# Moving the sums of an FFN's down weight blocks from one engine's queue to another's

## The reference, cut to what matters

```
def conv_ffn(x, norm_g, w_up, conv_w, conv_b, w_down):
    u = rmsnorm(x, norm_g) @ w_up                  # 256 x 5632
    ... # causal convolution of width 3 over positions
    val, gate = jnp.split(c, 2, axis=-1)
    return (jax.nn.silu(gate) * val) @ w_down      # (256 x 2816) @ (2816 x 1024)
```

## Time and profile before

| | us |
|---|---|
| median of 3 runs | 949.56 (948.84 to 949.63) |
| the profiled execution, its own time | 948.84 |
| its span, first to last instruction | 947.0 |
| PE busy | 936.0 (99%) |
| DVE busy | 799.8 (84%) |
| ACT busy | 278.2 (29%) |
| POOL busy | 0.7 (0%) |

### The profile page before, as it was taken

One profiled execution on the slowest core, in us unless ns is written; L12 is line 12 of the kernel. 1 busy time (PEld: TensorE's weight loads), 2 busy tenths in 40 slices (PEclk: granted clock), 3 DMA queues, 4 the chain that ended last, 5 costly groups with the idle time before them and its releaser, 6 DMA issues.

```text
span 947.0 us, 16131 instructions
## 1 busy us (share of the span) xinstructions
PE 936.0 (99%) x6456; PEld 865.2 (91%) x6456; DVE 799.8 (84%) x1822; ACT 278.2 (29%) x622; POOL 0.7 (0%) x7
## 2 busy tenths in 40 slices
PE   9999999999999999999999999999999999999997
PEld 7888999999999998889999999999888878888876
DVE  4778879999998878777699999988799985899953
ACT  1033122221212111263122221220424563624561
POOL 0000000000000000000000000000000000000000
PEclk9999999999999999999999999999999999999999
DMA  8942455363634650757254545446933428443101
GB/s 312 411 184 105 178 187 218 153 254 147 264 140 160 231 209 3 282 195 305 94 224 171 230 180 221 181 161 241 341 133 98 159 94 297 156 149 110 32 1 45
DMA packets 36859, 171.80 MB, mean 181 GB/s; under 512 B 5032, under 2 KB 8880, under 8 KB 23344
## 3 DMA queue, kind: packets, MB, share of 16 engines
q1 hardware_dynamic: 35120, 167.72, 47.7%
q10 hardware_dynamic: 1664, 3.04, 0.9%
HBM read 169.69 MB, written 2.64 MB: 182 GB/s over the span
## 4 chain that ended last, share of the span: by engine, by line
PE 92%; DVE 3%; DMA 2%; ACT 1%; issue 0%; ACTq 0%; SPq 0%; DVEq 0%
PE bank L1355 26%; PE bank L1375 15%; PE bank L1039 9%; PE bank L1458 5%; PE bank L1692 4%; PE bank L1108 3%; PE bank L1331 3%; PE bank L1301 3%; PE bank L1115 3%; PE bank L1678 3%; PE bank L1554 2%; PE bank L1573 2%; PE bank L1051 1%; PE bank L1498 1%; PE bank L1624 1%; DMA ring<-in_ring 1%
## 5 line engine op out<-in xcount | busy, mean ns | idle before, releaser
L1375 PE MATMUL bank<-work,fring 128*128 128x128 f32 x1008 | 115.5, 275 | 0.0
L1375 PEld LDWEIGHTS bank<-work,fring 128*128 128x128 f32 x1008 | 114.0, 192 | 0.0
L2514 DVE SCALAR_TENSOR_TENSOR work<-work,cols 128x256 f32<-128x256 f32 x240 | 98.8, 477 | 1.0 <-ACT work L893 0.5
L1355 PE MATMUL bank<-sq,fring 128*128 128x128 f32 x640 | 84.5, 275 | 0.0
L724 ACT ACTIVATE work<-work,cols 128x256 f32<-128x256 f32 x88 | 47.8, 593 | 111.0 <-DVE work L2237 96.2
L1355 PE MATMUL bank<-ring,fring 128*128 128x128 f32 x640 | 78.1, 275 | 0.0
L1355 PE MATMUL bank<-sq,ring 128*128 128x128 f32 x640 | 78.0, 275 | 0.0
L1355 PEld LDWEIGHTS bank<-sq,fring 128*128 128x128 f32 x640 | 77.9, 192 | 0.0
L1355 PEld LDWEIGHTS bank<-ring,fring 128*128 128x128 f32 x640 | 74.8, 192 | 0.2
L1355 PEld LDWEIGHTS bank<-sq,ring 128*128 128x128 f32 x640 | 74.7, 192 | 0.0
L2256 DVE SCALAR_TENSOR_TENSOR work<-work,cols 128x256 f32<-128x256 f32 x176 | 71.5, 477 | 0.0
(11 more groups left out here) (420 smaller groups left out, 1724.7 us busy)
## 6 DMA issues: line engine op xcount, KB each, us to landing
ring<-in_ring SPq DMA_DIRECT2D x60, 1024.0 KB, 6.9
fring<-in_up SPq DMA_DIRECT2D x44, 1024.0 KB, 6.8
ada_w<-in_ada SPq DMA_DIRECT2D x48, 512.0 KB, 6.3
fring<-in_down SPq DMA_DIRECT2D x44, 512.0 KB, 4.5
ring<-in_ring SPq DMA_DIRECT2D x2, 800.0 KB, 6.5
bias_skewed<-bias_rows SPq DMA_DIRECT2D x1, 1536.0 KB, 13.1
consts<-in_consts ACTq DMA_DIRECT2D x1, 1128.0 KB, 15.2
ring<-in_ring SPq DMA_DIRECT2D x2, 512.0 KB, 4.6
```

Source lines behind the costliest of these rows:

```text
L1355: last = mm(bank[:, P * at:P * (at + 1)], w[:, k, P * c:P * (c + 1)], x[:, k, :], start=(k == 0), stop=(k == 3))
L1375: last = mm(bank[:, at + P * c:at + P * (c + 1)], w[:, P * c:P * (c + 1)], x, start=(i == 0 and at == 0 and c == 0), stop=(i == FF_STEPS - 1),
L2514: marks[c] = link(v.scalar_tensor_tensor(b_y[:, c, :], b_a[:, c, tap:tap + T], col("conv_w_2", 124 * l + 4 * tap + c), b_y[:, c, :], ALU.m ...
```

## The change

The three instructions of `down_sums` move from DVE's program to POOL's, unchanged in operands and shapes. All 44 calls (22 in each FFN) go; POOL runs them in PE's order, each behind a wait for its DMA, with waits on a counter of its own (`down_step`) between dependent instructions. The four `ada(1)` of DVE's tail are now called together as `ada(4)`. The semaphores `c_in` and `gain_in` become one, `row_in`.

```diff
+            def down_sums(f, group, i):
+                no = down_no(f, group, i)
+                nc.gpsimd.wait_ge(S(down_landed(f, group, i)[0]), down_landed(f, group, i)[1])
+                w = down_place(f, group, i)
+                s1, vlo, glo, ghi, vhi, s2, s3, s4 = down_parts(f, group, i)
+                nc.gpsimd.tensor_tensor(s1, glo, ghi, ALU.add).then_inc(S("down_step"), 1)
+                nc.gpsimd.wait_ge(S("down_step"), 2 * no - 1)
+                nc.gpsimd.tensor_tensor(w[:, 1280:1792], w[:, 0:512], w[:, 256:768], ALU.subtract)\
+                    .then_inc(S("down_step"), 1)
+                nc.gpsimd.wait_ge(S("down_step"), 2 * no)
+                nc.gpsimd.tensor_tensor(s4, vhi, s2, ALU.subtract).then_inc(S("down_sums"), 1)
+
+            for f in range(2):
+                for i in range(FF_STEPS - 1):
+                    down_sums(f, 0, i)
+                down_sums(f, 1, 0)
+                down_sums(f, 1, 1)
+                down_sums(f, 0, FF_STEPS - 1)
+                for i in range(2, FF_STEPS):
+                    down_sums(f, 1, i)
...
-                def down_sums(group, i):
-
-                    dve.wait_ge(S(down_landed(f, group, i)[0]), down_landed(f, group, i)[1])
-                    w = down_place(f, group, i)
-                    s1, vlo, glo, ghi, vhi, s2, s3, s4 = down_parts(f, group, i)
-                    then(v.tensor_tensor(s1, glo, ghi, ALU.add))
-                    then(v.tensor_tensor(w[:, 1280:1792], w[:, 0:512], w[:, 256:768], ALU.subtract))
-                    v.tensor_tensor(s4, vhi, s2, ALU.subtract).then_inc(S("down_sums"), 1)
...
-                        else:
-                            down_sums(1, 0)
-                            down_sums(1, 1)
                         products_out(g, 1)
-                    down_sums(0, i)
                     taps(i, 0)
...
-                down_sums(1, 2)
-                down_sums(1, 3)
                 down_out(0)
                 for m in range(2):
-                    down_sums(1, 4 + m)
                     onward(m)
-                for i in range(6, FF_STEPS):
-                    down_sums(1, i)
-                    if i < 10:
-                        ada(1)
+                ada(4)
                 down_out(1)
```

More of the change, by code:

```diff
@@ L457, in _ @@
                 load(n)
-            sp.dma_start(c_row[:, :], I["c_2"][0].partition_broadcast(P)).then_inc(S("c_in"), 16)
+            sp.dma_start(c_row[:, :], I["c_2"][0].partition_broadcast(P)).then_inc(S("row_in"), 16)
             load_ada(0, 3)
@@ L513, in _ @@
             sp.wait_ge(S("gain_row_out"), 16)
-            sp.dma_start(gain_all, bass.AP(gain_row, 0, [[0, P], [1, D]])).then_inc(S("gain_in"), 16)
+            sp.dma_start(gain_all, bass.AP(gain_row, 0, [[0, P], [1, D]])).then_inc(S("row_in"), 16)
             for n, (b, lo, hi) in enumerate((b, lo, hi) for b in range(TB) for lo, hi in OUT_PARTS[b]):
@@ L735, in _ @@
             tables(SILU)
-            act.wait_ge(S("c_in"), 16)
+            act.wait_ge(S("row_in"), 16)
             nc.scalar.activation(c_row[:, :], c_row[:, :], ACT.Silu).then_inc(S("c_done"), 1)
@@ L2730, in layer @@
                         if l == 1:
-                            dve.wait_ge(S("gain_in"), 16)
+                            dve.wait_ge(S("row_in"), 32)
                             gained_out(b, 0)
```

## The result

| | before | after |
|---|---|---|
| median, us | 949.49 (948.84 to 949.63) | 957.33 (955.89 to 959.20) |
| ratio, 95% interval | | 1.0079 [1.0064, 1.0095] |
| the profiled execution: own time, span | 948.84, 947.0 | 955.89, 954.1 |

Five executions each. The change made the kernel 7.8 us slower, where the forecast was 949.4 us and the range ended at 956.5.

What follows compares the result with a forecast made beforehand. PE was taken to bound the kernel, busy 936.0 of 947.0 us. The only term was −0.15 us of PE waiting for DVE, so 949.56 − 0.15 = 949.4 us, with a range of 948.3 to 956.5.

Steps and rivals of the forecast that it cites:

- That PE bounds both FFNs, and the 0.15 us to gain: Both FFNs: PE runs without gaps, except one up product at 488.98 taking 12.66 us against 12.51.
- The price of a block on POOL: POOL's three sums per block: between 1.14 and 2.82 us, the upper taken, with waits 3.0 us.
- rival 3: POOL becomes the bound of the tails: at 5 us a block, 11 us in each tail, 971 us; chance 0.07.
- The 67 us off DVE: Over 44 blocks DVE loses 67 us of sums, 1.52 us in a step, leaving it busy near 733.
- the 1.93 us to spare in a step: FFN steps: DVE's slack against PE's 15.64 us step, 0.41 us before the change and 1.93 after.
- the sum: Whole kernel: only −0.15 us against the profiled 948.84; from the expected median 949.56 this gives 949.4 us.
- 2.24 us to spare: Start of each tail: the gated factor of step 10 precedes PE's need by 0.72 us, by 2.24 without the sums.
- Against it: Arguments against DVE and POOL blocking each other: POOL's hold may be only 1.7 us a block, or DVE keeps POOL out.
- rival 1: DVE and POOL take turns, PE stands at tail starts and ahead of the FFNs: 5.4 to 9.6 us, 956.9; chance 0.27.
- 2.8 us ahead of the FFNs: Before both FFNs: two POOL blocks delay DVE's sums for the out projection, so PE stands 1.7 and 1.1 us.
- In the middle of a step this would be harmless: Mid-step, POOL works 5.5 to 8.5 us into the up product, where DVE waits for PE and reads PSUM.
- the test that the prediction set for itself: Tail start: the prediction is wrong if DVE's chain from 298.5 to the gated factor exceeds its operations by over 2.2 us.

Runs made afterwards that it cites:

- the bare kernel: Nothing of the model computed: 24 DVE operations beside 8 of POOL or none; two-input DVE operations took 8.24 us alone, 16.78 beside POOL's additions.
- experiment 8: Two kernels, each the changed kernel plus one POOL wait: first, before (1,0) for step 9's gated factor, 955.58 us; second, before (1,2) for step 10's, 951.15 us.

## Why the prediction was wrong, point by point

- **That PE bounds both FFNs, and the 0.15 us to gain**: right. The up product fell from 12.66 to 12.51 us.
- **The price of a block on POOL**: right for a block that is left alone. 0.73, 1.33 and 0.79 us are the medians, against 0.73, 1.36 and 0.73, the upper bound that was taken, and about 3 us with the hops. The mean is 149 / 44 = 3.4 us of busy time, since POOL sometimes stands too. POOL was never late in after (rival 3 is out): loads were what it waited for.
- **The 67 us off DVE**: right as work, wrong as time. Without the reads of POOL DVE's busy time is 737 us (predicted 733); with them it is 793. Little of the 1.93 us to spare in a step appeared: the block shown above took back 2.0, and the mean block 1.26.
- **The step that failed** is the sum: "−0.15" and nothing else. It takes the 67 us off DVE and leaves all that DVE still does at its old length, so that step 10's factor has 2.24 us to spare. This term, put at nothing, measured 4.28 us from the taps to the factor in the first tail, and PE waited 3.10 and 1.80 us in the two tails where the forecast had 40.65 us without a wait. Behind the stalls came the fall of the clock, for which no line of the prediction has a term.
- **The grounds for putting it at nothing** stand under "Against it", and gave the forecast 0.61 and rival 1 0.27. The first was that POOL's hold might be shorter than its operation, 1.7 us a block. It was 2.0 for the block in the step above, 2.1 each for the two at the tail, and 1.07 us for each addition of 1.23 in the bare kernel. Besides, its sum doesn't come out: two blocks at 1.7 are 3.4 us, less 2.24 is up to 1.2 us in each tail, not "at most 0.4", and with two tails that is over the 1.9 us that counted as no change. The second ground was that DVE's close succession might keep POOL out instead. That happened (both tails of the execution of 951.05 us), but not as the rule: in three tails of ten.
- **Rival 1 itself** had the mechanism, the place, the two blocks and nearly the size: 1.3 to 3.4 us in each tail, measured 3.1 and 1.8, then 1.0 and 0.2 in another execution; 956.9 us in all, measured 957.3 and 955.8. That the total came so close is in part luck, as two errors offset. It charged 2.8 us ahead of the FFNs, where 0.28 at most came: POOL's first sums did stretch DVE's there, but not by the whole margin. And it had no term for the clock, 1.6 us in the profiled execution and an estimated 1.9 on average.
- **"In the middle of a step this would be harmless"**: right for PE, wrong for the reason. DVE wasn't waiting for PE when POOL worked; it was in `gated`, with two SBUF inputs. It was harmless because PE needed that factor much later.
- **The margin**: 2.24 us for step 10 was right, and the test that the prediction set for itself (DVE's chain from 298.5 to the factor more than 2.2 us longer than its operations) is what happened: 5.5 us later from 298.5 on, 4.3 of it in operations that took longer.
- **Missing from the prediction**: the blocks (1,0), (1,1) and (0,10) make POOL work from 287.0 to 297.6 us without a break, beside step 9. They made DVE 0.9 us late for step 10, which by itself, experiment 8 shows, costs nothing.
- The rule of the Trainium skill (SBUF — State Buffer, section "Who interferes with whom") that was weighed against the change held in every pair measured. The rows of before neither bore it out nor denied it, and a rule that states a measured mechanism, with a margin of 2.24 us against a delay worked out at 3.5 to 5.6, deserved more than 0.27.

## What to carry to other kernels

Before work is moved between DVE and POOL, list DVE's instructions with two SBUF inputs that will run beside it, and add POOL's whole length to each chain with a deadline; where a chain has less to spare than that, hold POOL back behind the chain's result, or leave these few pieces where they were. Taking instructions from an engine is no gain in itself: look for the place where the bound engine waits for it, and if there is none, the move can only lose. A short stall of PE may cost more than its length, since the granted clock can fall behind it.

## What the runs showed of the hardware

- A POOL addition of 512 columns (1.23 us) beside two-input SBUF operations of DVE costs DVE 1.07 us and POOL 0.15. For a copy (0.56 us) DVE pays 0.41, for a memset nothing, and nothing for anything if one of DVE's inputs is in PSUM.
- A DVE multiplication by a constant from SBUF, 0.21 us for 256 columns, is held up by all three, by 1.06, 0.41 and 0.40 us. It was the cheapest of the three instructions of DVE tried, and the only one that a memset held up.
- Who stands is settled anew at each meeting. In seven tails where POOL's first sum began up to 2.68 us behind the start of DVE's taps, DVE lost 1.5 to 2.5 us in taps and `ada`; in three where it began 2.75 us behind or later, POOL stood instead.
- The granted clock fell to half after stalls of PE of 3.1 us (after) and 2.6 us (experiment 8, first kernel), at a cost of 1.6 and 1.4 us, and did not after stalls of 1.8 us (after) and of 2.7 us twice (experiment 2, whose mean granted clock over seven executions is 0.9986). The stall's length alone therefore doesn't settle it; what else does is open.
